# Order of the 512- and 256-column products inside a weight tile, and other PSUM banks for the latent up projections and the keys' transposes

## The chip, the core and the metric

The kernel runs on one core of one Trainium2 chip. The metric is the device time of one execution in microseconds (us); the time of a kernel is the median of its runs. Engines are named as in the profile: PE is TensorE's matmul, PEld its weight load, DVE is VectorE, ACT is ScalarE, POOL is GpSimd, SP is SyncE.

## The reference

Two transformer blocks, one after the other, each with two layers, on 256 tokens of width 1024, all in float32.

The first block does in each layer: `proj = rms_norm(x) @ w_in`; a latent attention branch (`q = rms_norm(c_q) @ w_uq`, `kv = rms_norm(c_kv) @ w_ukv`, 8 heads, norms of the heads, rotary positions), a grouped-query attention branch (8 query heads, 2 key heads), a pooling branch; `merged` is the sum of the three, each times its own sigmoid gate; `x = x + merged @ w_out`; then `u = conv3(rms_norm(x) @ ffn_w_up)` and `x = x + (silu(u_gate) * u_val) @ ffn_w_down`, with 2816 hidden columns, so that `ffn_w_up` has 5632.

The second block does in each layer an attention (stick-breaking in layer 0, dilated in layer 1) with `w_in` and `w_out`, a feed-forward `relu(u @ w_ff_in)^2 @ w_ff_out` with 4096 hidden columns, and a gate with an embedding of the layer.

## The kernel before

**Products.** PE multiplies in the type fp32r. To keep float32's accuracy every operand is split into a high part (rounded) and a low part (the rest), and a product is made of three: high times high, high times low, low times high, all added in PSUM.

**Weight units.** The weights come as a list of units of up to 1024 floats for each partition (`weight_units`, L122). For each unit SP loads `w_raw` (L1072), ACT writes the high part `w_high` (L1696), DVE the low part `w_low` (L2208), and PE uses both. There are 6 places for split units and 4 for raw ones. PE waits for `w_low` of the unit at its start (L1269) and counts `w_used` at its end; ACT needs `w_used` of six units before to write a new high part.

**PSUM.** There are 8 banks of 512 floats. An accumulator is a slot of two neighbouring banks: slot 0 is banks 0 and 1, slot 1 is 2 and 3, slot 2 is 4 and 5, slot 3 is 6 and 7. `SLOTS` (L258) says which slots the panels of a linear take in turn. `acquire` (L1233) lets PE wait before it writes a bank until the last reader of the bank is done; who that is stands in `free`.

**Three forms of a unit on PE** (L1260 to L1315). In the token form (L1310, L1312, L1314) the features are the stationary operand and 512 columns of weights stream by: three matmuls into one bank for each block of 128 rows and each of the two token blocks. In the feature form (L1301, L1303, L1304) the weights are stationary and the 256 tokens stream by, also three matmuls. The third, the wide form (L1276 to L1292), is used for `ffn_up`, `sb_in` and `ff_in` but for the first panel of `ffn_up` and `ff_in`. Here high and low part of the features lie side by side, so that one matmul of 512 columns does high times high and high times low (L1283), and one of 256 columns does low times high (L1289). A unit is 256 weight columns by 4 blocks of 128 rows: 8 matmuls of 512 columns, one for each block and each half of the columns, and then 8 of 256 columns on the same places:

```
for j in range(u["nk"]):
    ... for f in range(w // P):
        eng.matmul(... wh[:, j, f * P:(f + 1) * P], parts ...)   # 512 columns
for j in range(u["nk"]):
    ... for f in range(w // P):
        eng.matmul(... wl[:, j, f * P:(f + 1) * P], high ...)    # 256 columns
```

**Order of the work.** One plan of steps (`Plan`, L311) gives the order in which every engine goes through its steps. Around the latent up projections PE does: the last unit of the first gates panel (`gates_early`, slot 1), the transposes of the keys (`g_turn_k`, L1407, 4 transposes into bank 4), the first panel of `up_q` (512 columns, slot 0), the transposes of the queries (`g_turn_q`, L1414, 8 transposes, four into bank 4 and four into bank 5), the second panel of `up_q` (256 columns, slot 1), the two panels of `up_kv` (slots 0 and 1), and the first scores (L1434, banks 4 and 5). On DVE the keys are copied out of bank 4 (L2372, by L2164), the gates panel is taken (L2422, two instructions), and half of the queries copied. ACT copies the other half (L1676) and takes the panels of `up_q` (`take_mq`, L1819) and `up_kv` (`take_mkv`, L1828 and L1829).

Of the kernel before, what the change touches and what calls it, by code (L numbers as in the profile page):

```python
# [14 lines left out]
P = 128  # L15
SEQ = 256
# [8 lines left out]
GQA_H, GQA_KV, HD = 8, 2, 64  # L25
# [15 lines left out]
PANEL = 512  # L41
# [208 lines left out]
def slot_of(name, layer, panel):  # L250
# [4 lines left out]
STAGE_SB, STAGE_DIL = 4, 7  # L255
STAGE_FF, STAGE_PLE = (5, 8), (6, 9)

SLOTS = {"proj": (0, 1, 2), "gates_early": (1,), "up_q": (0, 1), "up_kv": (0, 1), "gates": (0, 1),  # L258
         "branch_gqa": (1, 0), "branch_pool": (2, 3), "branch_mla": (1, 0), "out": (1, 0),
         "ffn_up": (2, 1, 3, 2) + 4 * (1, 0, 3, 2) + (1,), "ffn_down": (0, 1), "sb_in": (0, 1, 2), "sb_values": (2,), "sb_out": (2, 0),  # L260
         "dil_qk": (0, 1, 2, 0, 2, 1), "dil_values": (2,), "dil_out": (0, 2)}
# [611 lines left out]
class Kernel:  # L873
# [352 lines left out]
    def tensor(self, eng):  # L1226
# [14 lines left out]
        def turn_pairs(src, blocks, rows, banks, taken):  # L1241

            for n in range(0, blocks, 2):
                b = banks[(n // 2) % len(banks)]
                acquire(b)
                for i in range(2):
                    for t in range(TT):
                        o = i * SEQ + t * P
                        d = turn(bank[b][0:rows, o:o + P], src(n + i, t))
                free[b] = taken(n // 2)  # L1250
                d.then_inc(sem("pair_turned"), 1)
# [5 lines left out]
        for step in self.plan.steps:  # L1257
            kind, key = step[0], step[1:]

            if kind == "mm":  # L1260
                u = self.units[key[0]]
                w, kts = u["w"], KTS[u["name"]]
                s = slot_of(u["name"], u["layer"], u["panel"])
                acc = self.slot[s]

                blocks = key[1:] or tuple(range(TT))
                high, low = self.operands(u)
                wh, wl = (self.unit_view(a, u).rearrange("p (k n) -> p k n", n=w) for a in (self.wh, self.wl))
# [7 lines left out]
                if by_feature and u["name"] in WIDE:  # L1276

                    parts = self.wide_features(u)
                    for j in range(u["nk"]):
                        k = u["k0"] + j  # L1280
                        self.operand_ready(q, u, k, blocks[-1])
                        for f in range(w // P):
                            eng.matmul(acc[:, f * PANEL:(f + 1) * PANEL], wh[:, j, f * P:(f + 1) * P],  # L1283
                                       parts[:, k, :, :].rearrange("p s n -> p (s n)"), start=k == 0, stop=False,
                                       skip_group_check=True)
                    for j in range(u["nk"]):
                        k = u["k0"] + j
                        for f in range(w // P):
                            d = eng.matmul(acc[:, f * PANEL:f * PANEL + SEQ], wl[:, j, f * P:(f + 1) * P],  # L1289
                                           high[:, k, :], start=False, stop=k == kts - 1, skip_group_check=True)  # L1290
                    d.then_inc(sem("w_used"), 1)
                    continue  # L1292
                for j in range(u["nk"]):
                    k = u["k0"] + j
# [112 lines left out]
            elif kind == "g_turn_k":  # L1407
                l, = key
                kd = self.mix[l]["kd"]
                q.wait_ge(sem("g_k_rotated"), at("g_rot_k", l))  # L1410
                turn_pairs(lambda n, t: kd[:, t, n, :, :], GQA_KV, P, (4,),
                           lambda n: (sem("g_k_taken"), at(*step)))

            elif kind == "g_turn_q":  # L1414
# [741 lines left out]
    def vector(self, eng):  # L2156
# [4 lines left out]
        def copy_pair(step, banks, rows, out, n, done, scale=1.0):  # L2161
            q.wait_ge(sem("pair_turned"), self.plan.pair_end[step] - self.plan.pairs(step) + n + 1)
            b = banks[n % len(banks)]
            ts(out[0:rows, 2 * n:2 * n + 2, :], bank[b][0:rows, :].rearrange("p (k s) -> p k s", k=2), scale, None,  # L2164
               ALU.mult).then_inc(sem(done), 1)
# [34 lines left out]
        for step in self.plan.steps:  # L2200
# [168 lines left out]
                rotate(tile, GQA_H, HD, self.mix[l]["tgq"], [tile], "g_q_rotated")  # L2369

            elif kind == "g_turn_k":
                copy_pair(step, (4,), P, self.mix[key[0]]["gh"][:, 4:6, :], 0, "g_k_taken")  # L2372

            elif kind == "g_turn_q":
                copy_pair(step, (4, 5), P, self.mix[key[0]]["gh"][:, 0:4, :], 0, "g_q_taken_dve")
# [598 lines left out]
```

## Time and profile before

| what | value |
|---|---|
| median of 3 runs | 1479.62 us (1478.97 to 1479.88) |
| the profiled execution's own time | 1479.08 us |
| its span, first to last instruction | 1477.2 us |
| granted TensorE clock, mean | 1.000 |
| PE busy | 1467.3 us (99%), 7790 matmuls |
| PEld busy | 1234.6 us (84%) |
| DVE busy | 1102.1 us (75%) |
| ACT busy | 885.0 us (60%) |
| DMA packets, share of 16 engines | 54.8% |

Of the span 1.9 us of the profiled execution's own time lie outside. The ends of matmuls are modelled, and a matmul's row is longer than the time until the next one starts, since they are pipelined. What a matmul costs is therefore read from the distance between the starts of two, not from its duration. A row of the timeline that says x8 holds eight matmuls of one line; the distance from its start to the start of the next row is what the eight cost.

### The profile page before, as it was taken

Reading aid. Unit: us, or ns where it says so; the run is one execution under the profiler, and the core shown is the slowest. Engines: PE = TensorE matmul, PEld = TensorE weight load, DVE = VectorE, ACT = ScalarE, POOL = GpSimd, SP = SyncE. Lnnn points to the kernel's source line nnn. Section 1 sums busy time; section 2 is a strip of 40 time slices with the busy share of each in tenths; the row PEclk is TensorE's granted clock in tenths of the full one; section 3 lists DMA queues with packets and bytes.
Section 4 is the critical chain, followed back from the end, with each engine's and each line's share of the span. In section 5 each row is a group of like instructions: output and inputs, shape, how many; then the busy total and the mean of one; then the engine's idle time right before and its main releaser. Section 6 shows DMA issues by size and latency. Waiting matters only on the chain.

```text
span 1477.2 us, 20112 instructions
## 1 busy us (share of the span) xinstructions
PE 1467.3 (99%) x7790; PEld 1234.6 (84%) x7790; DVE 1102.1 (75%) x1674; ACT 885.0 (60%) x1348; POOL 57.1 (4%) x69
## 2 busy tenths in 40 slices
PE   9999999999999999999999999999999999999998
PEld 7877788888897778888888877888888888888887
DVE  7898779996578978799956667875467567887446
ACT  7555657775447565677744576664456455666435
POOL 0110000000021000000000001000010000100001
PEclk9999999999999999999999999999999999999999
DMA  8643546666555335566666523756646544556662
GB/s 300 204 131 114 162 152 199 188 198 195 176 165 181 132 114 174 169 190 198 188 194 197 179 92 119 229 187 194 192 158 237 163 124 137 166 198 191 194 188 84
DMA packets 74015, 256.75 MB, mean 174 GB/s; under 512 B 8640, under 2 KB 9920, under 8 KB 73920
## 3 DMA queue, kind: packets, MB, share of 16 engines
q1 hardware_dynamic: 73776, 255.46, 54.8%
q8 instruction: 62, 1.02, 0.3%
q14 instruction: 33, 0.27, 0.1%
q10 hardware_dynamic: 144, 0.00, 0.0%
HBM read 254.38 MB, written 1.05 MB: 173 GB/s over the span
## 4 chain that ended last, share of the span: by engine, by line
PE 92%; DVE 4%; ACT 2%; DMA 1%; issue 1%; POOL 1%; DVEq 0%; ACTq 0%
PE psum L1283 19%; PE psum L1310 18%; PE psum L1312 18%; PE psum L1314 18%; PE psum L1289 10%; PE psum L1239 4%; PE psum L1454 2%; DVE w_low L2208 1%; PE psum L1484 1%; PE psum L1541 1%; DMA w_raw<-in_weights 1%; ACT w_high L1696 1%; PE psum L1591 0%; PE psum L1623 0%; PE psum L1526 0%
## 5 line engine op out<-in xcount | busy, mean ns | idle before, releaser
L2208 DVE TENSOR_TENSOR w_low<-w_raw,w_high 128x1024 fp32r<-128x1024 f32 (+2 forms) x482 | 573.8, 1198 | 206.8 <-ACT w_high L1696 205.8
L1696 ACT ACTIVATE w_high<-w_raw 128x1024 fp32r<-128x1024 f32 (+2 forms) x482 | 498.9, 1038 | 252.5 <-PE psum L1314 219.7
L1283 PE MATMUL psum<-x_parts,w_high 128*128 128x512 f32 x992 | 248.8, 393 | 0.0
L1283 PEld LDWEIGHTS psum<-x_parts,w_high 128*128 128x128 f32 x992 | 178.6, 189 | 32.2
L1310 PE MATMUL psum<-w_high,x_parts 128*128 128x512 f32 (+2 forms) x432 | 170.0, 394 | 1.3 <-DVE w_low L2208 0.7
L1312 PE MATMUL psum<-w_low,x_parts 128*128 128x512 f32 (+2 forms) x432 | 164.0, 380 | 0.0
L1314 PE MATMUL psum<-w_high,x_parts 128*128 128x512 f32 (+2 forms) x432 | 163.9, 379 | 0.0
L1289 PEld LDWEIGHTS psum<-x_parts,w_low 128*128 128x128 f32 x992 | 135.3, 190 | 9.7
L1289 PE MATMUL psum<-x_parts,w_low 128*128 128x256 f32 x992 | 138.3, 282 | 0.0
L1310 PE MATMUL psum<-w_high,ff_high 128*128 128x512 f32 x256 | 99.8, 390 | 0.0
L1312 PE MATMUL psum<-w_low,ff_high 128*128 128x512 f32 x256 | 99.6, 389 | 0.0
L1314 PE MATMUL psum<-w_high,ff_low 128*128 128x512 f32 x256 | 99.6, 389 | 0.0
L1310 PEld LDWEIGHTS psum<-w_high,x_parts 128*128 128x128 f32 x432 | 81.3, 188 | 21.0 <-issue 5.0
L1314 PEld LDWEIGHTS psum<-w_high,x_parts 128*128 128x128 f32 x432 | 81.2, 188 | 15.2
L1312 PEld LDWEIGHTS psum<-w_low,x_parts 128*128 128x128 f32 x432 | 81.4, 188 | 13.1
L1310 PE MATMUL psum<-w_high,x_parts_next 128*128 128x512 f32 (+1 forms) x208 | 79.3, 381 | 0.6 <-DVE x_parts_next L2260 0.6
L1314 PE MATMUL psum<-w_high,x_parts_next 128*128 128x512 f32 (+1 forms) x208 | 77.6, 373 | 0.0
L1312 PE MATMUL psum<-w_low,x_parts_next 128*128 128x512 f32 (+1 forms) x208 | 77.5, 373 | 0.0
L1310 PE MATMUL psum<-w_high,ffn_high 128*128 128x512 f32 x176 | 68.7, 390 | 0.0
L1312 PE MATMUL psum<-w_low,ffn_high 128*128 128x512 f32 x176 | 68.5, 389 | 0.0
L1314 PE MATMUL psum<-w_high,ffn_low 128*128 128x512 f32 x176 | 68.5, 389 | 0.0
L1310 PE MATMUL psum<-w_high,mixed_high 128*128 128x512 f32 (+1 forms) x152 | 60.0, 395 | 0.5 <-DVE gates L2422 0.3
(282 smaller groups left out, 2323.2 us busy)
## 6 DMA issues: line engine op xcount, KB each, us to landing
w_raw<-in_weights SPq DMA_DIRECT2D x450, 512.0 KB, 3.9
w_raw<-in_weights SPq DMA_DIRECT2D x16, 384.0 KB, 3.1
w_raw<-in_weights SPq DMA_DIRECT2D x7, 416.0 KB, 3.7
rows<-in_second_rows SPq DMA_DIRECT2D x4, 512.0 KB, 4.9
w_raw<-in_weights SPq DMA_DIRECT2D x6, 256.0 KB, 2.7
scratch<-in_x_turned SPq DMA_DIRECT2D x4, 256.0 KB, 4.7
residual<-in_x SPq DMA_DIRECT2D x2, 512.0 KB, 6.8
dil_masks<-in_consts SPq DMA_DIRECT2D x1, 768.0 KB, 6.1
```

The lines of the kernel that those rows point to most:

```text
L1239: return eng.transpose(out, src, ident)
L1283: eng.matmul(acc[:, f * PANEL:(f + 1) * PANEL], wh[:, j, f * P:(f + 1) * P], parts[:, k, :, :].rearrange("p s n -> p (s n)"), start=k == 0 ...
L1289: d = eng.matmul(acc[:, f * PANEL:f * PANEL + SEQ], wl[:, j, f * P:(f + 1) * P], high[:, k, :], start=False, stop=k == kts - 1, skip_group ...
L1310: eng.matmul(o, high[:, k, cut], wh[:, j, :], start=k == 0, stop=False, skip_group_check=True)
L1312: eng.matmul(o, high[:, k, cut], wl[:, j, :], start=False, stop=False, skip_group_check=True)
L1314: d = eng.matmul(o, low[:, k, cut], wh[:, j, :], start=False, stop=end, skip_group_check=True)
L1454: d = eng.matmul(bank[4 + i][:, t * SEQ:(t + 1) * SEQ], qt[i][:, t * P:(t + 1) * P], kt[i], start=True, stop=True)
L1484: d = eng.matmul(bank[6][HD * i:HD * i + HD, 0:SEQ], val, m["probt"][i][:, kt * SEQ:(kt + 1) * SEQ], start=kt == 0, stop=kt == TT - 1, ski ...
L1541: d = eng.matmul(o, m, r, start=False, stop=True, skip_group_check=True)
L1696: act(self.unit_view(self.wh, u), raw, ACT.Copy).then_inc(sem("w_high"), 1)
L2208: tt(self.unit_view(self.wl, u), raw, self.unit_view(self.wh, u), ALU.subtract).then_inc(sem("w_low"), 1)
```

## The change

In the wide form the 256-column product now stands directly behind the 512-column product of the same tile of weights. It still uses the same operands, writes the same columns and is counted in the same way, at the unit's end. `ffn_up`, `sb_in` and `ff_in` use this form. Besides, the panels of `up_q` take slots 0 and 3 in place of 0 and 1, those of `up_kv` slots 1 and 3 in place of 0 and 1, and the keys are transposed into bank 6 in place of bank 4, with their copy on DVE reading from there.

```diff
-SLOTS = {"proj": (0, 1, 2), "gates_early": (1,), "up_q": (0, 1), "up_kv": (0, 1), "gates": (0, 1),
+SLOTS = {"proj": (0, 1, 2), "gates_early": (1,), "up_q": (0, 3), "up_kv": (1, 3), "gates": (0, 1),
...
                         for f in range(w // P):
-                            eng.matmul(acc[:, f * PANEL:(f + 1) * PANEL], wh[:, j, f * P:(f + 1) * P],
+                            cut = slice(f * P, (f + 1) * P)
+                            eng.matmul(acc[:, f * PANEL:(f + 1) * PANEL], wh[:, j, cut],
                                        parts[:, k, :, :].rearrange("p s n -> p (s n)"), start=k == 0, stop=False,
                                        skip_group_check=True)
-                    for j in range(u["nk"]):
-                        k = u["k0"] + j
-                        for f in range(w // P):
-                            d = eng.matmul(acc[:, f * PANEL:f * PANEL + SEQ], wl[:, j, f * P:(f + 1) * P],
-                                           high[:, k, :], start=False, stop=k == kts - 1, skip_group_check=True)
+                            d = eng.matmul(acc[:, f * PANEL:f * PANEL + SEQ], wl[:, j, cut], high[:, k, :],
+                                           start=False, stop=k == kts - 1, skip_group_check=True)
...
-                turn_pairs(lambda n, t: kd[:, t, n, :, :], GQA_KV, P, (4,),
+                turn_pairs(lambda n, t: kd[:, t, n, :, :], GQA_KV, P, (6,),
                            lambda n: (sem("g_k_taken"), at(*step)))
...
-                copy_pair(step, (4,), P, self.mix[key[0]]["gh"][:, 4:6, :], 0, "g_k_taken")
+                copy_pair(step, (6,), P, self.mix[key[0]]["gh"][:, 4:6, :], 0, "g_k_taken")
```

## Rows read from the trace of the kernel before

**Rows 1.** Busy time of each engine, with its share of the span and instructions.

```profile
PE 1467.3 (99%) x7790; PEld 1234.6 (84%) x7790; DVE 1102.1 (75%) x1674; ACT 885.0 (60%) x1348; POOL 57.1 (4%) x69
```

**Rows 2.** Groups of instructions: matmuls of the wide form | busy, mean ns | idle before.

```profile
L1283 PE MATMUL psum<-x_parts,w_high 128*128 128x512 f32 x992 | 248.8, 393 | 0.0
...
L1283 PE MATMUL psum<-x_parts_next,w_high 128*128 128x512 f32 x224 | 56.2, 393 | 0.0
```

**Rows 3.** Timeline of PE in `ffn_up`, layer 0: start us, length us, what.

```profile
230.82 2.00 PE L1283 MATMUL psum<-x_parts,w_high 128*128 128x512 f32 x8
232.66 1.11 PE L1289 MATMUL psum<-x_parts,w_low 128*128 128x256 f32 x8
...
334.17 2.00 PE L1283 MATMUL psum<-x_parts,w_high 128*128 128x512 f32 x8
```

**Rows 4.** Timeline of PE: two long runs, 512 columns in `ff_out`, 256 in `proj`.

```profile
1003.00 0.39 PE L1314 MATMUL psum<-w_high,ff_low 128*128 128x512 f32 x1
...
1090.05 0.40 PE L1314 MATMUL psum<-w_high,ff_low 128*128 128x512 f32 x1
...
34.30 0.28 PE L1303 MATMUL psum<-x_parts,w_high 128*128 128x256 f32 x1
...
45.58 0.28 PE L1304 MATMUL psum<-x_parts,w_low 128*128 128x256 f32 x1
```

**Rows 5.** Timeline: where the width of the products changes, with one weight load.

```profile
45.70 0.40 PE L1310 MATMUL psum<-w_high,x_parts 128*128 128x512 f32 x1
45.70 0.19 PEld L1312 LDWEIGHTS psum<-w_low,x_parts 128*128 128x128 f32 x1
45.93 0.40 PE L1312 MATMUL psum<-w_low,x_parts 128*128 128x512 f32 x1
...
46.17 0.39 PE L1314 MATMUL psum<-w_high,x_parts 128*128 128x512 f32 x1
...
407.61 0.40 PE L1310 MATMUL psum<-w_high,x_parts 128*128 128x512 f32 x1
...
408.76 0.39 PE L1314 MATMUL psum<-w_high,x_parts 128*128 128x512 f32 x1
...
418.51 0.28 PE L1310 MATMUL psum<-w_high,x_parts 128*128 128x256 f32 x1
418.62 0.28 PE L1312 MATMUL psum<-w_low,x_parts 128*128 128x256 f32 x1
```

**Rows 6.** Stretch 231 to 334 us: us busy by engine (instructions), clock, DMA, GB/s.

```profile
231.00:334.00 103.00, 103.00 (x591) 90.60 (x591) 98.16 (x143) 76.64 (x105) 0.00 (x0) 1.00 0.63 189
```

**Rows 7.** Timeline around the up projections, layer 0: PE, then DVE, then ACT.

```profile
59.61 0.39 PE L1314 MATMUL psum<-w_high,mixed_low 128*128 128x512 f32 x1
60.15 1.06 PE L1239 MATMUL psum<-consts,gqa_tokens 128*128 128x128 f32 x8 [0.16 <-DVE gqa_heads L2164]
61.47 0.35 PE L1310 MATMUL psum<-w_high,mixed_high 128*128 128x256 f32 x1 [0.25 <-DVE gates L2422]
...
64.36 0.45 PE L1310 MATMUL psum<-w_high,mixed_high 128*128 128x512 f32 x1
...
59.32 0.68 DVE L2164 TENSOR_SCALAR gqa_heads<-psum 128x512 f32<-128x512 f32 x1
59.92 1.40 DVE L2422 TENSOR_SCALAR gates<-psum,stat 128x512 f32<-128x512 f32 x2
...
61.25 0.60 ACT L1676 ACTIVATE gqa_heads<-psum 128x512 f32<-128x512 f32 x1 [3.31 <-PE psum L1239]
...
63.60 0.60 ACT L1819 ACTIVATE mla_tokens<-psum 128x512 f32<-128x512 f32 x1
```

**Rows 8.** Timeline around the up projections, layer 1: PE, then ACT.

```profile
453.68 0.47 PE L1310 MATMUL psum<-w_high,mixed_high 128*128 128x512 f32 x1 [0.22 <-issue]
...
455.16 0.47 PE L1310 MATMUL psum<-w_high,mixed_high 128*128 128x512 f32 x1
...
454.41 0.60 ACT L1819 ACTIVATE mla_tokens<-psum 128x512 f32<-128x512 f32 x1
```

## The prediction, made before the changed kernel was run

> **What bounds the kernel now.** I read the busy times first: PE is busy for 99% of the span, the next engine for 75% [rows 1]. So the time is the sum of what the matmuls cost, plus a few microseconds of waits, and a change pays only if matmuls follow each other more closely or if one of the waits goes. A busy row does not tell the first, since matmuls overlap; I read distances between starts in the timeline.
>
> The groups by line give 992 + 224 = 1216 matmuls of 512 columns in the wide form [rows 2], at 8 for each unit 152 units, and as many matmuls of 256 columns. In `ffn_up` of layer 0 the unit that starts at 230.82 and the one at 334.17 are 37 units apart: 103.35 / 37 = 2.793 us for a unit, of which the eight 512-column matmuls take 1.84 and the eight others the remaining 0.95 [rows 3]. The groups show no idle time before these matmuls [rows 2]: no wait is left in this stage, and the unit's price is PE's own.
>
> The stretch view says what stands beside it. Between 231 and 334 us DVE is busy for 98.2 of 103 us, ACT for 76.6, the DMA share is 0.63, and the granted clock is 1.00, which is the 2.4 GHz level [rows 6]. DVE has some 5% of room there.
>
> **The order of the products.** No matmul, weight load, DMA or semaphore is added or removed; DVE, ACT, SP and POOL issue what they did. The waits of the wide form stay where they are (the unit's `w_low` and banks at its start), and `w_used` still comes with the unit's last matmul. Inside a unit the wait for the features of a block comes behind the 256-column products of the earlier blocks, thus later: nobody gets a new wait by it. What changes is which matmul follows which. Before there is one step from 512 to 256 columns in a unit and one back; afterwards there are eight of each.
>
> The price of a matmul in a long run: in `ff_out` the starts at 1003.00 and 1090.05 are 384 matmuls apart, 0.2267 us each; in `proj` the 256-column starts at 34.30 and 45.58 are 94 apart, 0.1200 us each [rows 4]. A unit at these prices is 8 x (0.2267 + 0.1200) = 2.774 us. It costs 2.793. The missing 0.02 us lies at the steps. Eight 512-column matmuls at the run's price are 1.81, in the unit they take 1.84 [rows 3, 4]. The same is seen elsewhere: after the 256-column run of `proj` the first two 512-column matmuls cost 0.235 each (45.70 to 46.17); after products of 416 columns the first five cost 1.15 in place of 1.13 (407.61 to 408.76); and in the other direction the first 256-column matmul costs 0.11 in place of 0.12 (418.51 to 418.62) [rows 5]. So a step up costs, a step down gives a little back, and the stream needs about five matmuls to settle. The whole lead is 0.02 us a unit, and the question is what becomes of a disturbance that takes five matmuls when the width changes at every matmul.
>
> The trace of before has no alternating stream, so I bound it. Cheapest: a 256-column product always costs the 0.113 of a first one (0.95 less seven of 0.12), and the 512-column one its 0.2267: 0.340 for the pair. Dearest: the 512-column one always costs the 0.235 of a first one, the other 0.120: 0.355. I take 0.3467, the two long-run prices, because they are the best supported rows (384 and 94 matmuls) and because the 0.235 and the 0.113 look like two ends of one shift: what the first narrow product gives, the first wide one takes back. That is 2.774 a unit, 0.0196 less, times 152 = 3.0 us less. A weight load beside it does not change this: it starts together with the matmul before (both at 45.70) and lasts 0.19 [rows 5], and in the 256-column run it is overlapped to the same degree. Two matmuls on one bank in succession cost nothing either: the token form puts three on one bank and has the 0.2267.
>
> **The banks.** Layer 0. The query transposes start at 60.15, held up by the copy of the keys out of bank 4, which ends at 59.32 + 0.68 = 60.00; the matmul before started at 59.61 [rows 7]. With the keys in bank 6 they start at 59.61 + 0.23 = 59.84, 0.31 earlier. The second `up_q` panel starts at 61.47, held up by the gates that DVE reads out of slot 1 until 61.32 [rows 7]. In slot 3 it needs the keys' copy (60.00), and starts right behind the transposes, some 0.7 earlier. Not all of that stays: the second `up_kv` panel starts at 64.36 and needs in either kernel that ACT has taken the second `up_q` panel, now at 63.60 + 0.60 = 64.20. ACT comes to it by way of the copy at 61.25, which waits for the query transposes [rows 7]. So this chain moves by the 0.31, and 0.31 is what is left. The first `up_kv` panel, now in slot 1, needs the gates of 61.32, and would start near 62.3: the new wait is covered, by 1 us.
>
> Layer 1. The wait before 453.68, for slot 0, goes; but the second `up_kv` panel at 455.16 waits for ACT's 454.41 + 0.60 = 455.01 in slot 1 now and in slot 3 later [rows 8]. Nothing is left of it. What is late next is in both layers ACT's reading of the second `up_q` panel. Sum for the banks 0.3 us, at most 0.7 if ACT's chain turned out shorter, at worst nothing; a loss would need the later probability transposes in banks 6 and 7 to wait for ACT's reading of `up_kv`, which lies whole units of gates earlier.
>
> **Sum.** 3.0 + 0.3 = 3.3 us less: 1479.08 becomes 1475.8 for the profiled execution, which lies 0.5 below the median of the runs; against the median of 1479.6 it is 1476.3.
>
> **Rivals.**
>
> *The narrow product becomes cheap.* If the 0.12 of the narrow run is set by the weight loads, which a 256-column product barely covers, then alternation puts each of these loads under a product with room, and the pair costs 0.340: 2.720 a unit, 0.073 less, 11.1 us, with the banks 1468.2. For it: the first narrow product behind a wide one costs 0.11 [rows 5]. Against it: a load under the narrow product is still needed before each wide one, so one of the two stays where it was; and in this stretch DVE has to do 98.2 us of work in what would be 100.6 [rows 6]. The Trainium skill (TensorE: Matmul & The Clock Gate, section Back-to-back issue gap) says that in a stream the spacing is set by load and matmul together; by that rule this rival's mechanism exists, and no row here separates it from a fixed extra for each matmul.
>
> *The step up is paid at every pair (slower).* Place: the wide product behind a narrow one, 1216 times. Price: 0.235 in place of 0.2267, while the narrow one does not drop below 0.120. The pair costs 0.355, the unit 2.840, 0.047 more, 7.1 us, with the banks 1486.4. It decides from a pair of 0.3491 on (2.793 / 8), that is from a 512-column product of 0.229. For it: the extra after 416 columns is as large as after 256 [rows 5], as if the step alone counted. Against it: with one narrow product in between there is little to recover from.
>
> *The order makes no difference.* The extra is spread over the pairs, some 0.0025 each, and the unit stays at 2.793; only the banks are left: 1479.3. The Trainium skill has a rule that leads here (the same page, section Part 3: Packing small matmuls): a weight load overlaps a running matmul only if it goes to another row group. By it every load of the full array would stand alone, whatever the order. The trace does not agree: load and matmul both start at 45.70 [rows 5]. The rival stands without it, on the spread alone.
>
> **How the numbers follow.** A measurement of this kernel tells about 0.2% (3 us) from no change. Long-run prices: 0.42. Its time lies on that border, so I give 0.25 of it to faster, 0.17 to the same. Cheap narrow product: 0.22, faster. Step paid at every pair: 0.22, slower. No difference: 0.14, of which 0.04 would still come out faster with some of the gain. Faster 0.51, the same 0.27, slower 0.22. The predicted time is that of the likeliest case, 1476.3. The range goes from the cheap case, 1468, to the dear one, 1486.5; the likeliest case's own range is 1475 to 1478.
>
> **What would show it.** In the profile afterwards the wide units of `ffn_up` must lie 2.774 us apart; single starts in the pair should read 0.227 (or 0.233) and 0.120 (or 0.113). 2.72 means the first rival, 2.84 the second, 2.793 the third. Around 60 us the query transposes should start near 59.84 without a wait for the keys, the second `up_q` panel near 60.7, the second `up_kv` panel near 64.05; in layer 1 that panel still at the same distance from ACT's reading. The forecast is wrong if the unit is not within 0.01 of 2.774, or if a wait for DVE or ACT appears before the wide matmuls, where there is none now.

## The result: slower, by 0.3%

| | before | changed kernel |
|---|---|---|
| median | 1479.48 us (7 runs, 1478.97 to 1479.91) | 1484.02 us (7 runs, 1483.13 to 1484.20) |
| span of the profiled execution | 1477.2 us | 1482.3 us |
| 152 wide units, in sum | 425.39 us | 430.22 us |

The ratio is 1.0030, with a 95% interval from 1.0021 to 1.0039. The forecast was 1476.3 us and faster; the result is slower than before by 4.5 us, inside the range (1468 to 1486.5), but near its dear end. The sum of the wide units is, for each of the 152 units, the distance from its first start to the start of the matmul behind its last one. It is the number by which all runs below are compared. Below, a time given without a number of runs is that of one execution.

**Where the time went.** The spans differ by 5.1 us. I subtracted the starts of the same matmul (the n-th of the program) in the two traces: 0.50 us come in the first 26 us, before any changed instruction, where PE waits for the first weights; 0.31 us are given back at the latent up projections of layer 0; nothing changes in those of layer 1; 4.83 us come inside the wide units, and some 0.1 elsewhere. The 0.50 at the start is scatter and no effect of the change: from the first matmul to the 101st the traces of this case take 24.9 to 25.7 us, with either order and either banks. Without it, 4.83 - 0.31 = 4.52 us are left, which is the difference of the medians (4.54).

The busy times after the change answer to [rows 1]: PE is busy for 5.3 us more, the other engines for at most 1.1 us more.

```profile
PE 1472.6 (99%) x7790; PEld 1233.9 (83%) x7790; DVE 1102.5 (74%) x1674; ACT 886.1 (60%) x1348; POOL 57.2 (4%) x69
```

The groups, without a wait as in [rows 2]:

```profile
L1284 PE MATMUL psum<-x_parts,w_high 128*128 128x512 f32 x992 | 351.2, 399 | 0.0
L1287 PE MATMUL psum<-x_parts,w_low 128*128 128x256 f32 x992 | 278.5, 281 | 0.0
```

The stretch from 231 to 334 us answers to [rows 6]: the clock is granted in full (1.00, the 2.4 GHz level), DVE has more room than before (97.1 of 103 us, since fewer units fit in).

```profile
231.00:334.00 103.00, 103.00 (x585) 89.39 (x584) 97.10 (x141) 75.69 (x103) 0.00 (x0) 1.00 0.61 187
```

So it is neither a wait, nor the clock, nor DVE: the matmuls themselves lie further apart. The timeline of PE in the changed kernel, in `ffn_up` of layer 0 and, at the end, in `sb_in`, with the columns of [rows 3]:

```profile
231.09 0.40 PE L1284 MATMUL psum<-x_parts,w_high 128*128 128x512 f32 x1
...
233.93 0.40 PE L1284 MATMUL psum<-x_parts,w_high 128*128 128x512 f32 x1
234.16 0.28 PE L1287 MATMUL psum<-x_parts,w_low 128*128 128x256 f32 x1
234.28 0.40 PE L1284 MATMUL psum<-x_parts,w_high 128*128 128x512 f32 x1
...
234.62 0.40 PE L1284 MATMUL psum<-x_parts,w_high 128*128 128x512 f32 x1
234.87 0.28 PE L1287 MATMUL psum<-x_parts,w_low 128*128 128x256 f32 x1
234.99 0.40 PE L1284 MATMUL psum<-x_parts,w_high 128*128 128x512 f32 x1
...
335.69 0.40 PE L1284 MATMUL psum<-x_parts,w_high 128*128 128x512 f32 x1
...
796.26 0.39 PE L1284 MATMUL psum<-x_parts,w_high 128*128 128x512 f32 x1
796.49 0.28 PE L1287 MATMUL psum<-x_parts,w_low 128*128 128x256 f32 x1
796.61 0.39 PE L1284 MATMUL psum<-x_parts,w_high 128*128 128x512 f32 x1
...
797.99 0.39 PE L1284 MATMUL psum<-x_parts,w_high 128*128 128x512 f32 x1
```

The unit at 231.09 and the one at 335.69 are 37 apart: 2.827 us each, where the forecast said 2.774 and [rows 3] have 2.793. From 233.93 to 234.99 three pairs take 1.06 us, 0.3533 a pair, and the same three repeat: the wide product costs 0.233, 0.241, 0.236 in turn, the narrow one 0.117, 0.120, 0.113. But from 796.26 to 797.99 five pairs take 1.73 us, 0.346 a pair, in the same kernel and the same loop: the price that the forecast took. Two prices for one stream; this became the question.

The up projections of layer 0, PE and then ACT, and of layer 1, PE and then ACT, answer to [rows 7, 8]. The whole layer lies 0.50 later here; less that, the query transposes start at 59.84 and the second `up_kv` panel at 64.00:

```profile
60.11 0.39 PE L1312 MATMUL psum<-w_high,mixed_low 128*128 128x512 f32 x1
60.34 1.03 PE L1239 MATMUL psum<-consts,gqa_tokens 128*128 128x128 f32 x8
61.13 0.36 PE L1308 MATMUL psum<-w_high,mixed_high 128*128 128x256 f32 x1
...
64.50 0.47 PE L1308 MATMUL psum<-w_high,mixed_high 128*128 128x512 f32 x1 [0.30 <-ACT mla_tokens L1817]
...
63.76 0.60 ACT L1817 ACTIVATE mla_tokens<-psum 128x512 f32<-128x512 f32 x1
...
456.73 0.47 PE L1308 MATMUL psum<-w_high,mixed_high 128*128 128x512 f32 x1 [0.30 <-ACT mla_tokens L1817]
...
455.98 0.60 ACT L1817 ACTIVATE mla_tokens<-psum 128x512 f32<-128x512 f32 x1
```

In both layers the second `up_kv` panel starts 0.14 to 0.15 us behind the end of ACT's reading (64.36 and 456.58); before it was 0.15 to 0.16.

### The profile page after: what moved, and what is told of

Its sections match the earlier page's. It is cut to its first block, busy times and chain, and to the rows that moved or that the text cites. A ratio compares the mean times of both kernels' runs of the same rounds, so it can differ in the third digit from the quotient of the medians.

```text
span 1482.3 us, 20110 instructions
## 1 busy us (share of the span) xinstructions
PE 1472.6 (99%) x7790; PEld 1233.9 (83%) x7790; DVE 1102.5 (74%) x1674; ACT 886.1 (60%) x1348; POOL 57.2 (4%) x69
## 4 chain that ended last, share of the span: by engine, by line
PE 95%; DVE 2%; ACT 2%; DMA 0%; issue 0%; SPq 0%; ACTq 0%; DVEq 0%
PE psum L1284 19%; PE psum L1308 19%; PE psum L1312 18%; PE psum L1310 18%; PE psum L1287 10%; PE psum L1239 4%; PE psum L1452 2%; PE psum L1482 1%; PE psum L1539 1%; DVE w_low L2206 1%; ACT w_high L1694 1%; PE psum L1299 1%; PE psum L1301 1%; PE psum L1302 1%; DMA w_raw<-in_weights 0%; PE psum L1589 0%
## 5 line engine op out<-in xcount | busy, mean ns | idle before, releaser
L1284 PE MATMUL psum<-x_parts,w_high 128*128 128x512 f32 x992 | 351.2, 399 | 0.0
L1287 PE MATMUL psum<-x_parts,w_low 128*128 128x256 f32 x992 | 278.5, 281 | 0.0
L1284 PEld LDWEIGHTS psum<-x_parts,w_high 128*128 128x128 f32 x992 | 186.4, 188 | 46.0
L1287 PEld LDWEIGHTS psum<-x_parts,w_low 128*128 128x128 f32 x992 | 187.4, 189 | 0.2
L1284 PE MATMUL psum<-x_parts_next,w_high 128*128 128x512 f32 x224 | 79.4, 399 | 0.0
```

The costliest lines, as they stand in the source:

```text
L1284: eng.matmul(acc[:, f * PANEL:(f + 1) * PANEL], wh[:, j, cut], parts[:, k, :, :].rearrange("p s n -> p (s n)"), start=k == 0, stop=False, ...
L1287: d = eng.matmul(acc[:, f * PANEL:f * PANEL + SEQ], wl[:, j, cut], high[:, k, :], start=False, stop=k == kts - 1, skip_group_check=True)
```

## The experiments

The edits are named against the changed kernel or against the one before. "Banks of before" means the three other lines of the diff undone.

**The two parts apart.** The first has only the new order, the second only the new banks.

> The new order of the products alone, with the banks of before. Theory A (the order is the whole loss, and it lies inside the wide units): the wide units take 430.2 us in sum as in the changed kernel, against 425.4 before, +4.8 us, and the time is about 1484.3. Theory B (the banks or the arrival of the first weights carry a part): less than +4 us. In a unit most pairs repeat with three different costs (0.349, 0.350, 0.361 us, sum 1.060), some stretches with 0.347 each.

1483.94 us (6 runs), ratio 1.0031, 1.0020 to 1.0042; wide units 430.23 us in sum. The whole loss is the order's.

> The new banks alone, with the order of before. Theory A: the second up_kv panel of layer 0 starts 0.31 us earlier, in layer 1 at the same place, and the time falls by 0.3 us to about 1479.2, within the noise. Theory B (the banks cost something elsewhere): the time rises by 1 us or more.

1479.00 us (11 runs), ratio 0.9999, 0.9990 to 1.0007; wide units 425.41. Matmul by matmul against before, the trace has gained 0.34 us by the 400th matmul (at 76 us, behind the up projections of layer 0) and gains nothing behind it. That is the step as forecast, too small for the medians to show. The traces of all runs bear on it. From the 250th to the 400th matmul all eleven with the new banks take 30.42 us, and seven of the eight with the banks of before 30.70 to 30.89. The eighth is the run with the order alone: it takes 30.37, since there the query transposes follow at once, without the wait for the keys' copy. The timeline of PE in that run:

```profile
59.74 0.39 PE L1312 MATMUL psum<-w_high,mixed_low 128*128 128x512 f32 x1
59.98 0.27 PE L1239 MATMUL psum<-consts,gqa_tokens 128*128 128x128 f32 x1
```

So the new banks take away a wait that most executions have, but not all.

**Fewer changes of width, not more.** In this run the second unit of each panel does its narrow products first (one line of the edit):

```diff
+                    todo = [(n,) + tile for n in ((1, 0) if u["k0"] else (0, 1)) for tile in tiles]
```

> The new banks, and a third order: the first unit of a panel does its eight 512-column products and then its eight of 256, the second unit its eight of 256 first and then its eight of 512. That has one step up in width for each two units where before had one for each. If a step up costs 20 ns (the difference of 2.793 and 2.773), two units take 5.566 in place of 5.587, 76 times 0.020 = 1.5 us less, with the banks 1477.7. If the loss of 20 ns comes from something else in a unit (its waits, its start), it stays and only the banks' 0.3 us are seen: 1479.2.

1477.75 us (11 runs), ratio 0.9988, 0.9979 to 0.9997. The timeline of PE has sixteen of each kind in turn:

```profile
240.29 3.82 PE L1291 MATMUL psum<-x_parts,w_high 128*128 128x512 f32 x16
243.94 2.08 PE L1288 MATMUL psum<-x_parts,w_low 128*128 128x256 f32 x16
245.86 0.40 PE L1291 MATMUL psum<-x_parts,w_high 128*128 128x512 f32 x1
```

Two units take 5.57 us in place of 5.587 and hold one step up in place of two; nominal are 5.547. So a single step up does cost 0.02 us, the lead of the forecast. The wide units fall by 1.35 us in sum, to 424.04. Next, more steps: with the banks of before, two wide products and two narrow ones in turn (four steps up a unit), and four and four (two steps). The line of the first:

```diff
+                    todo = [(n, j, f) for j in range(u["nk"]) for n in (0, 1) for f in range(w // P)]
```

> Banks of before; in each block of rows two products of 512 columns (both halves) and then two of 256: four steps up in a unit, where before has one and the changed kernel eight. If every step up costs the same 20 ns: 2.773 + 4 x 0.020 = 2.853 a unit, +9 us. If a loss of 20 ns comes every third step up, as the changed kernel's repeating triple says: 2.773 + 4/3 x 0.020 = 2.80, +1 us. If it depends on how far the stream has settled: between.

1478.38 us (8 runs), ratio 0.9994, 0.9984 to 1.0004; wide units 424.49 us. Two unit starts, 37 units apart, give 2.787 us a unit:

```profile
231.15 0.40 PE L1290 MATMUL psum<-x_parts,w_high 128*128 128x512 f32 x1
...
334.26 0.40 PE L1290 MATMUL psum<-x_parts,w_high 128*128 128x512 f32 x1
```

> Banks of before; four products of 512 columns, then four of 256, twice in a unit: two steps up. Seen so far over 2.773: one step up with runs of eight 20 ns, four steps with runs of two 13 ns, eight steps with runs of one 58 ns or none. If a step up costs a full settling when the run in front of it is long enough (four is): 2.813 a unit, +3 us. If each step costs 3 ns as with runs of two: 2.780, 2 us less.

1481.11 us (8 runs), ratio 1.0011, 0.9999 to 1.0022; wide units 427.16 us. Again 37 units apart, 2.807 us a unit:

```profile
230.87 0.40 PE L1291 MATMUL psum<-x_parts,w_high 128*128 128x512 f32 x1
...
334.72 0.40 PE L1291 MATMUL psum<-x_parts,w_high 128*128 128x512 f32 x1
```

Neither time is clear of the kernel before; the units are. The extra over 2.773 is 10 ns a unit at half a step up, 20 at one, 33 at two, 13 at four and 53 at eight: the cost does not go by the number of steps. Each short pattern has its own price.

**Is it the bank?** In the changed kernel the narrow product writes the bank that the wide one before it wrote. Here it belongs to the tile before, thus to the other bank (banks of before; the lines that add the first and the last product of a unit are not shown):

```diff
+                    for last, tile in zip(tiles, tiles[1:]):
+                        todo += [(0,) + tile, (1,) + last]
```

> Banks of before; widths alternate as in the changed kernel, but the 256-column product belongs to the tile before, so it writes another bank than the 512-column product in front of it. Theory S (the step in width makes the loss): the same as the changed kernel, three costs in turn, 0.353 a pair, 152 units 430 us. Theory P (two products on one bank in succession make the loss): 0.3467 a pair, 152 units 421.5 us, 3.9 us less than before.

1483.09 us; a unit 2.820 us, wide units 428.96. A unit begins with two wide products and ends with two narrow ones, so it has seven steps up. From one wide start at 240.34 to the next but one, the timeline shows 0.35 and 0.36, as in the changed kernel:

```profile
240.34 0.40 PE L1293 MATMUL psum<-x_parts,w_high 128*128 128x512 f32 x1
240.57 0.28 PE L1290 MATMUL psum<-x_parts,w_low 128*128 128x256 f32 x1
240.69 0.40 PE L1293 MATMUL psum<-x_parts,w_high 128*128 128x512 f32 x1
...
241.05 0.40 PE L1293 MATMUL psum<-x_parts,w_high 128*128 128x512 f32 x1
```

The extra does not need the narrow product on the bank of the wide one before it. But the edit only moves the shared bank: here each wide product writes the bank of the narrow one before it. That a bank written twice in succession costs nothing by itself is shown by the run with 512 beside 512 columns below, and the orders by twos and by fours, which never do it, have extras too. Pairs without any such succession were not tried.

**Is it the weight load, or the alternation as such?** Three runs, banks of before, widen the narrow product. In the first two it has 384 columns of the two feature parts side by side, in the order of before and in pairs; in the third 512 columns, in pairs. They add more of the low part of the weights than the kernel's sum has, so their outputs are other numbers, and their times are to be held against their own nominal values.

In short:

```diff
-  eng.matmul(acc[:, f * PANEL:f * PANEL + SEQ], wl[:, j, cut], high[:, k, :], ...)
+  eng.matmul(acc[:, f * PANEL:f * PANEL + 3 * P], wl[:, j, cut], parts(k)[:, 0:3 * P], ...)
```

> Order of before, but the product with the low part of the weights takes 384 columns in place of 256 (it adds a part that does not belong there, so the result is another one); a load of 0.12 us is well covered by such a product, which costs 0.1733 in long runs. Theory S: still a loss at the step up, some 20 ns a unit: 8 x (0.2267 + 0.1733) + 0.02 = 3.22. Theory L (a narrow product that hardly covers the weight load makes the loss): 3.200 without a rest, and the first 512-column products at 0.2267.

1550.87 us; a unit 3.267 us, 67 ns over 3.200, that is 8 x (0.2267 + 0.1733). The 0.1733 is also the price of a long run in the kernel before, in the dilated attention; these starts are 19 matmuls apart:

```profile
1233.81 0.33 PE L1312 MATMUL psum<-w_low,x_parts_next 128*128 128x384 f32 x1
...
1237.10 0.34 PE L1314 MATMUL psum<-w_high,x_parts_next 128*128 128x384 f32 x1
```

The extra did not shrink with the longer product over the load, it became three times as large. But the 0.12 us that the expectation gives for a load is the spacing in the run of 256 columns; the load's own row lasts 0.188 us (mean), so that 384 columns still do not cover it.

> The same 384-column product, in the order of the changed kernel (again another result than the reference's). Theory S: a pair above 0.400, the unit above that of the runs if it goes as with 256 columns. Theory L: 0.400 a pair and 3.200 a unit, no difference to the runs.

1554.01 us. The timeline of PE in `ffn_up`:

```profile
239.71 0.40 PE L1290 MATMUL psum<-x_parts,w_high 128*128 128x512 f32 x1
239.94 0.34 PE L1287 MATMUL psum<-x_parts,w_low 128*128 128x384 f32 x1
240.12 0.40 PE L1290 MATMUL psum<-x_parts,w_high 128*128 128x512 f32 x1
...
240.53 0.40 PE L1290 MATMUL psum<-x_parts,w_high 128*128 128x512 f32 x1
...
241.36 0.40 PE L1290 MATMUL psum<-x_parts,w_high 128*128 128x512 f32 x1
```

Four pairs take 1.65 us, 0.413 a pair and 3.307 a unit. In the `ff_in` stretches of the same trace a unit is 3.253:

```profile
1018.34 0.39 PE L1290 MATMUL psum<-x_parts,w_high 128*128 128x512 f32 x1
...
1021.59 0.39 PE L1290 MATMUL psum<-x_parts,w_high 128*128 128x512 f32 x1
```

Two prices again, 53 ns apart as in the changed kernel.

> Control: the order of the changed kernel, but the product with the low part of the weights takes 512 columns too (it adds a part that does not belong there; another result than the reference's). High and low weights and the two products still alternate, only the width does not. If the width is what costs: 0.2267 for every one, a unit of 3.627 us. If the alternation of the weights' tiles or the succession on one bank costs: above 3.65.

1605.68 us. The timeline of PE, 37 units apart:

```profile
232.69 0.39 PE L1290 MATMUL psum<-x_parts,w_high 128*128 128x512 f32 x1
...
366.88 0.39 PE L1290 MATMUL psum<-x_parts,w_high 128*128 128x512 f32 x1
```

134.19 / 37 = 3.627 us is sixteen times 0.2267, with nothing over: same alternation of weights, lines and operands, but one width. So neither the alternation nor the shared bank costs anything by itself. Two things went at once, though: the change of width, and the products that are shorter than the row of a load (0.188 us). The extra that grows from 256 to 384 columns speaks for the width, and so does the step up from 416 columns: it costs the same 0.02 us as the one from 256 [rows 5], though these products lie 0.187 us apart, nearly a load's row. But no run has two widths that both cover a load, so that the load as a part of the cause is not excluded.

**Does a stretch keep the price it starts with?** Each of the four `ffn_up` and `ff_in` stretches has near its start a break with eight transposes of features: behind its first unit in `ffn_up`, behind its second in `ff_in`, where another break with four small matmuls stands behind the first. These runs repeat the last of the eight transposes 1, 2 or 4 times (4, 8 or 16 transposes in the program, 0.11 us each): work that changes nothing in the result, and nothing in the wide loop.

```diff
                         d = turn(self.slot[s][:, o:o + P], src[:, t, i * P:(i + 1) * P])
+                for _ in range(1):
+                    d = turn(self.slot[s][:, o:o + P], src[:, t, i * P:(i + 1) * P])
```

> The changed kernel, with the last of the transposes in front of the long wide stretches (ffn_up from its second unit on, ff_in of layer 0 and 1) done once more: 0.11 us of work for each of three or four places. One stretch of the changed kernel ran at 0.347 a pair (the units at 797.99 and before) and the others at 0.353, with nothing different in them. If the state at the start decides and then holds, one more transpose may put a stretch into the 0.347 state: its units read 2.773 in place of 2.83. If the 0.353 is the stream's own price, all units stay at 2.82 to 2.83.

1477.23 us: more work, and 6.8 us less than the changed kernel.

> As the run before, with two more transposes in place of one. Same expectations: by stretch either 2.773 or 2.83, and which one is decided at the start of the stretch, if the state theory holds; 2.83 throughout if not.

1480.29 us.

> As the two runs before, with four more transposes in place of one or two. Same expectations: by stretch either 2.773 or 2.83 if the state theory holds, and 2.83 throughout if not.

1483.95 us. The five wide stretches, in us, with three runs told of further down (the second execution with one repeated transpose, three repeated, and the last row):

| kernel | ffn_up 0 | ffn_up 1 | sb_in | ff_in 0 | ff_in 1 | sum |
|---|---|---|---|---|---|---|
| before | 111.79 | 111.79 | 45.09 | 78.37 | 78.35 | 425.39 |
| changed | 113.12 | 113.12 | 45.48 | 79.24 | 79.25 | 430.22 |
| 1 repeated | 111.06 | 111.06 | 45.48 | 77.88 | 77.87 | 423.36 |
| 1, second execution | 111.06 | 111.06 | 45.48 | 77.87 | 77.89 | 423.36 |
| 2 repeated | 111.06 | 111.06 | 45.48 | 79.24 | 79.24 | 426.09 |
| 3 repeated | 113.13 | 113.13 | 45.48 | 79.25 | 79.24 | 430.23 |
| 4 repeated | 113.14 | 113.14 | 45.48 | 77.88 | 79.24 | 428.88 |
| first unit by runs | 113.08 | 113.08 | 44.90 | 79.24 | 77.87 | 428.18 |

A stretch of `ffn_up` takes one of two values, 111.06 or 113.1, one of `ff_in` 77.88 or 79.24, and nothing between. `sb_in` has a second break inside, with scores at 804 us, and there the price can change: in the changed kernel the three units from 795 to 803 us are cheap (2.773 for the undisturbed one), the twelve behind the break dear (2.82 to 2.83 but for the first, 2.903). The unit between the two breaks of `ff_in` is cheap there too (2.858, with the gap of a break in it). The time of the kernel follows from how many stretches are at which price.

**Is it so in every execution, and is the order needed?** The kernel with one repeated transpose, timed, and its control with the order of before.

> The changed kernel with one transpose repeated ahead of each long wide stretch, as in the single look before, now timed. State theory, and the state is fixed by the instructions ahead of the stretch: every run comes out like the look, 1477.2 +- 0.6 us, about 6.8 us under the changed kernel and 2.3 under the kernel before; the five long stretches of the trace again 111.06, 111.06, 45.48, 77.88, 77.87 us, to 0.05. Rival, chance: the state is drawn anew in each execution, so that single runs scatter over 1477 to 1484 us and the stretches of this trace come out in another mix than in the look.

1477.58 us (11 runs, 1476.62 to 1477.96), ratio 0.9986, 0.9978 to 0.9995; stretches as in the execution above, to 0.02. The two executions were on different chips. The timeline of PE shows the break and the stream behind it:

```profile
227.05 1.15 PE L1239 MATMUL psum<-consts,scratch 128*128 128x128 f32 x9
...
230.12 0.39 PE L1284 MATMUL psum<-x_parts,w_high 128*128 128x512 f32 x1
230.35 0.28 PE L1287 MATMUL psum<-x_parts,w_low 128*128 128x256 f32 x1
...
230.81 0.39 PE L1284 MATMUL psum<-x_parts,w_high 128*128 128x512 f32 x1
231.04 0.28 PE L1287 MATMUL psum<-x_parts,w_low 128*128 128x256 f32 x1
...
333.43 0.39 PE L1284 MATMUL psum<-x_parts,w_high 128*128 128x512 f32 x1
```

102.62 / 37 = 2.773 us a unit, 0.230 and 0.117 in the pair. The rival, chance in each execution, falls: eleven runs lie within 1.4 us, where the two ends are 7 apart, and both traces have every stretch at the same price.

> Control: the banks of the change, the order of before (eight wide products, then eight narrow ones), with the same repeated transposes. State theory: only the alternating stream has two states, so the repeated transposes cost here what they last, 0.1 us each or some 0.5 in all, and the kernel comes to 1479.0 to 1479.7 us, the 152 wide units to 425.4 us in sum, as without them. Rival: the repeated transposes help any order (a gap closed, a load or a wait hidden ahead of the stretch): then this kernel too falls by over 2 us, to 1477 or less, and its wide units to under 424.

1479.42 us (10 runs), ratio 1.0000, 0.9991 to 1.0009; wide units 425.36. The repeated transposes do not help the order of before. A break leaves a trace there too, but it ends with the unit behind: in the kernel before, the unit behind the eight transposes takes 2.881 us in `ff_in` of layer 0 and 2.866 in layer 1, and the next ones 2.793 in both.

> The changed kernel with three repeated transposes ahead of each long wide stretch. One and two gave the 2.773 us unit in both ffn_up stretches, four the 2.83 one; in ff_in one gave 2.773 in both, two 2.83 in both, four one of each. If the state went by odd and even counts, three would do as one: about 1477 us, wide sum 423.4. If it goes by how far the stretch is shifted (the first ones good, later ones bad), ffn_up may come out either way and three tells nothing of one. Either way each long stretch must be at one of its two values (111.06 or 113.1; 77.88 or 79.24), not between; a value between them, or a third one, speaks against two states.

1485.34 us. The count goes neither by odd and even nor by a threshold: none, three and four leave `ffn_up` at the dear price, one and two do not. Both values of each stretch are the known ones.

**What picks the price?** Two runs enter the alternating stream from a fixed run of eight narrow products: in the first at every second unit, in the second only in the first unit of each stretch (ahead of the transposes). The lines of the first:

```diff
+                    if not u["k0"]:
+                        todo = [(n,) + tile for n in (0, 1) for tile in tiles]
```

> Changed kernel, but the first unit of each wide panel in the order of before (eight wide products, then eight narrow ones), the second in pairs: each pair unit is entered from eight narrow products. Theory A, the way into the alternating stretch fixes its state: all 76 pair units come out alike, at 2.773 us (wide sum 76 x (2.793 + 2.773) = 423.0 us, kernel about 1476.7) or at 2.82 to 2.83 (427.2, kernel about 1481). Theory B, the state goes by something further back or by chance: both kinds of pair units within the trace, stretch by stretch as in the changed kernel. In no case a unit between 2.78 and 2.81, but for those behind a break.

1480.42 us, wide units 427.04. The timeline of PE around one unit of each kind:

```profile
239.01 0.40 PE L1292 MATMUL psum<-x_parts,w_high 128*128 128x512 f32 x1
...
239.72 0.40 PE L1292 MATMUL psum<-x_parts,w_high 128*128 128x512 f32 x1
...
240.78 0.40 PE L1292 MATMUL psum<-x_parts,w_high 128*128 128x512 f32 x1
...
241.84 1.99 PE L1292 MATMUL psum<-x_parts,w_high 128*128 128x512 f32 x8
243.67 1.11 PE L1289 MATMUL psum<-x_parts,w_low 128*128 128x256 f32 x8
244.62 0.40 PE L1292 MATMUL psum<-x_parts,w_high 128*128 128x512 f32 x1
```

241.84 - 239.01 = 2.83 us for the unit in pairs, 244.62 - 241.84 = 2.78 for the one in runs. By the starts to 1 ns it is 2.775, in place of the 2.793 of before, though its own sixteen products stand in the same order: behind one narrow product instead of eight, the first wide one costs 0.235 and the others 0.227 at once. So not even the 0.02 of a step up is fixed. Of the 76 units in pairs, 71 take 2.831 or 2.832 us; the other five stand at a break and are longer (2.90 to 3.03). None is at 2.773. Entered from a run of eight narrow products the stream is dear, in all of them. The same holds behind a steady run of wide ones: the first unit of each stretch in the changed kernel follows such a run and starts with 0.226, 0.114, 0.232, 0.118, 0.241, 0.120, the dear three. With 384 columns it is the other way: behind the same wide run the first unit of each of the five stretches is cheap (0.231 and 0.175 in turn).

> Changed kernel, but the first unit of each of the five wide stretches in the order of before, all others in pairs. Theory A, the way into the alternating stretch fixes its state, which then holds: the five stretches come out alike, all at 2.773 us a unit (wide sum about 422.3 us, kernel 1476) or all near 2.83 (430.2, kernel 1484), and like the pair units of the run before this one. Theory B, state by something further back: the stretches differ among each other (say 111.1 for one ffn_up stretch and 113.1 for the other).

1482.20 us. The stretches differ (last line of the table): `ff_in` of layer 1 is cheap, the one of layer 0 dear, though each is entered from the same unit and the same transposes. In `sb_in` it is now the other way round than in the changed kernel: dear up to the break at 804 us (2.831), cheap behind it (2.773 or 2.774). So it is a break, not the run ahead of it, from which this stream came out cheap where it did. What decides it stays open. The rows hardly tell the cases apart: in the changed kernel the eight transposes and the gap behind them take 0.790 us ahead of the cheap units at 795.13 and 0.791 ahead of the dear ones at 228.19, and in the run with the order alone 0.790 stands ahead of cheap ones in `sb_in` and of dear ones in `ffn_up` of layer 1. A finer difference in timing would be a guess.

## Why the prediction was wrong, point by point

**What bounds the kernel** was right: PE's own spacing, no wait behind it, DVE with room.

**The banks** were right: 0.31 us forecast, 0.31 in the changed kernel and 0.34 with the banks alone, at the query transposes (59.84 forecast, 60.34 - 0.50 read), and nothing in layer 1, for the reason given, ACT's reading of the second `up_q` panel. That the keys' wait is there to be taken was read from one trace; one of eight with the old banks has none. The second `up_q` panel, without its wait for the gates, starts at 61.13 - 0.50 = 60.63 (60.7 forecast), and that lead is lost again as said.

**The order** failed, at this step: "I take 0.3467, the two long-run prices, because they are the best supported rows", with the argument that "what the first narrow product gives, the first wide one takes back". 0.3467 exists, to 0.1 ns: 2.773 us a unit in `sb_in` at 797.99 and in four stretches of the kernel with one repeated transpose. But it is one of two prices, and the stream as written mostly falls into the other: 0.3533, or 2.827 a unit, 34 ns above the 2.793 of before instead of 20 below. The prediction's own sign of being wrong, a unit not within 0.01 of 2.774, is met. In the sum, 152 x 0.0196 = 3.0 us less became 4.8 us more. The warning was in the text, "the stream needs about five matmuls to settle": a price measured in steady runs says nothing of a stream that never becomes steady, and the prediction went back to the steady rows because there were many of them.

**The step up is paid at every pair** came nearest: slower, 1486.4 against 1484.0, a pair of 0.355 against 0.3533, above its own deciding point of 0.3491. Its mechanism is only half right, so that coming near is partly luck. The narrow product keeps on average 0.1167, not 0.120, and the wide one costs 0.2367; and the cost does not go with the steps, since four steps a unit cost less (13 ns) than one (20) or two (33). It would also have forbidden the cheap state.

**The narrow product becomes cheap** was wrong: no unit in pairs comes to 2.72, in either state.

**The order makes no difference** was wrong in the time, and its spread of the extra has no row: no steady unit of the changed kernel is at 2.793.

What is shown: the extra is there for 256 and 384 beside 512 columns and not for 512 beside 512, it grows rather than shrinks from 256 to 384, it does not need the narrow product on the bank of the wide one before, it has two values for one stream, and the value held until the next break. That the change of width is the cause is the likelier reading, not shown: a part of the weight load is not excluded. What stays open: what at a break picks the value, and what in TensorE makes the difference of 20 ns in three pairs. No run varied what stands at a break more finely than by one transpose (0.11 us). That the changed kernel lands in the dear state in `ffn_up` and `ff_in` is therefore no property of its order alone.

## What to carry to other kernels

A price read from long runs of equal matmuls does not hold for a stream of changing widths; time the very pattern, over a stretch, before it is spread over 1200 pairs. The safe orders here were those with one price in all stretches: sixteen of each (wide units 424.04 us, 1477.75 with the banks) and two of each (424.49, a time not clear of before), while pairs gave 1477.6 or 1484.0 by what stood ahead of them. And if an edit shifts a PE-bound kernel by some 0.1 to 0.5%, look at the spacing of the matmuls it did not touch: one repeated transpose in each of four breaks moved this kernel by 6.4 us.

## What the runs showed of the hardware that was not expected

- The stream of 512- and 256-column products in turn has two steady states at the same granted clock of 1.00: 0.3467 us a pair (0.230 and 0.117, or 0.231, 0.113, 0.232, 0.118 in turn, as in `sb_in` of the last run) and 0.3533 (a cycle of three pairs, 1.060 us). With 384 in place of 256 columns they are 0.4067 and 0.4133. Both times the difference is 6.7 ns a pair.
- From a run of either width the stream of 512 and 256 columns enters the dear state each time seen (71 units behind eight narrow products, five behind wide ones); the cheap one appeared only behind a break, where matmuls of other forms and a short gap stand between. The stream of 512 and 384 enters the cheap one behind wide products, five times of five.
- Equal products have no extra: 512 columns cost 0.2267 us in a long run, whether high and low weights alternate at every product or not.
- The price of a pattern isn't monotonic in its changes of width: 10, 20, 33, 13 and 53 (or 0) ns a unit for one step up in two units, one, two, four and eight in a unit. The Trainium skill (TensorE: Matmul & The Clock Gate, section Back-to-back issue gap) has the spacing in a stream set by weight load and matmul together; these orders have the same loads, but not the same product over each, so the differences between them don't speak against the rule. What it doesn't give is two prices for one and the same order.
